# One function table for exponential and logarithm, and a state-space stage that carries a state from block to block

## The chip, the cores and the metric

The kernel runs on one core of a Trainium2 chip. It is one program of 33,089 instructions. The metric is the device time in microseconds, the median of several runs. The kernel before took 2977.17 us (three runs, 2975.21 to 2984.87). The execution that the hardware profiler recorded took 2977.9 us, and its span, from the first instruction to the last, is 2976.1 us. Engines are named as in the profile: PE (TensorE, matrix products), PEld (its weight loads), DVE (VectorE), ACT (ScalarE), POOL (GpSimd), SP (SyncE, which asks for the transfers).

## The reference, cut to what matters

Three blocks run one after the other on 512 tokens of width 1024: attention with a gated network, a convolution with a retention layer, and a block that has an mLSTM branch and a state-space branch. The change touches the state-space branch in its structure, and in the others only where exponentials and logarithms are taken. The state-space branch has 16 heads of width 64 in 4 groups, and a state of 128:

```python
def ssd_chunked(x, dt, A, Bm, Cm):          # x (B,T,16,64), dt (B,T,16), Bm/Cm (B,T,4,128)
    xc = x * dt[..., None]                  # all in chunks of tokens
    a_cs = jnp.cumsum(dt * A, -1)           # within a chunk
    cb = jnp.einsum('bclgn,bcsgn->bgcls', Cc, Bc)
    mix = cb[:, :, None] * segsum_exp(a)    # exp(a_cs[l] - a_cs[s]) for s <= l, else 0
    y_diag = jnp.einsum('bgrcls,bcsgrp->bclgrp', mix, xc)
    decay_to_end = exp(a_cs[..., -1:] - a_cs)
    states = jnp.einsum('bcsgn,bcsgrp->bcgrpn', Bc, xc * decay_to_end[..., None])
    # h_prev of a chunk = exp(a_cs[-1]) * h_prev of the one before + its states
    y_off = jnp.einsum('bclgn,bcgrpn->bclgrp', Cc, h_prev) * exp(a_cs)[..., None]
    return y_diag + y_off
# then y + d_skip * x, and the rest of the branch
```

Softmax, the stick-breaking weights (a softplus, so a logarithm of one plus an exponential), every norm (the inverse root is taken as exp(-0.5 log v)) and the mLSTM gates use exponential and logarithm in turn.

## The kernel before

All activations lie in on-chip memory as 128 channels by 512 tokens, and the weights stream through. The core of the program is `weights_part` (its loops are in the function that holds lines 960 to 1119): a list of steps, each a run of weight tiles of 256 columns or a `Part`, a piece of program for some engines. Every engine walks this list in the same order. For a tile, SP asks for 1 MB of weights (L970), POOL splits it into a rounded part and a rest (L1024, L1030), PE multiplies it in three products (L1077, 48 matmuls of 512 columns), and DVE and ACT take the result out of one of two accumulators (banks 0 to 3) and free it (L1005). POOL may run two tiles ahead of PE, and PE one tile ahead of DVE and ACT.

`conv_tiles` takes a tile of the state-space input out: DVE applies four taps (L2109, L2111), ACT adds the bias and a SiLU (L2132). There are four such tiles for the values (chunks 16 to 23 of A), then the small tile of the time steps with `steps_parts`, then four tiles for the keys (B, chunks 24 to 27) and queries (C, 28 to 31). `steps_parts` is a chain between DVE and ACT (softplus, four running sums from four starting points, their rounded parts and rests).

Then comes the state-space stage between `meeting`s, points at which PE, ACT and DVE wait for each other (L162). `mamba_inputs_part` transposes the values (PE, L1922) and multiplies them by the time step (DVE, L1932, 64 instructions of 64 columns). `mamba_part` treats the 512 tokens in four key blocks of 128, and each block meets all later queries: 512, 384, 256 and 128 columns. For every head and block, PE spreads the running sums and adds the mask (L1957, L1960), ACT takes the exponential (L2000), DVE multiplies by the group's scores, which lie in banks 0 to 3 (L2010), and PE multiplies with the values (L1969, fp32). The scores of a group are L1977, the end of a head pair is L2015. The order on PE is written out by hand: the products of a head stand after the second block of the next head.

ACT holds one table of functions at a time; the program loads one (ACT_TABLE_LOAD) whenever the function at hand isn't in it. The loads of the kernel before choose one table for Exp and another for Ln.

Of the kernel before, what the change touches and what calls it, by code (L numbers as in the profile page):

```python
# [23 lines left out]
P = 128  # L24
# [20 lines left out]
CONST_SQ = ["ident", "ones", "rot", "diff_mask", "strict", "strict_neg", "neg_upper", "neg_ones", "causal_neg"]  # L45

# [566 lines left out]
class EarlyNorm:  # L613
# [42 lines left out]
    def scalar(self, act):  # L656
# [16 lines left out]
        act.activation(st.small[:, 15:16], st.eps_col(self.eps), ACT.Ln)  # L673
# [536 lines left out]
def attention_part(nc, st):  # L1210
# [120 lines left out]
    def _(act):  # L1331
# [49 lines left out]

        for h in range(SH):
            softplus(h)
            if h:
                copy_wt(2 * h - 1)
                if h % 2 == 0:
                    head_square(h // 2 - 1)
            exps(2 * h)
            if h and h % 2 == 0:
                copy_pair(h // 2 - 1)  # L1390
            attend(h)
            copy_wt(2 * h)
            exps(2 * h + 1)
            if h and h % 2 == 0:
                head_rstd(h // 2 - 1)
# [116 lines left out]
def retention_part(nc, st, t):  # L1512
# [38 lines left out]
    def _(act):  # L1551
        for h in range(RET_HEADS):
# [48 lines left out]
def gates_parts(nc, st, rows_ready):  # L1601
# [42 lines left out]
    def _(act):  # L1644
        act.wait_ge(biased, 1)
# [20 lines left out]
def mlstm_part(nc, st):  # L1666
# [74 lines left out]
    def _(act):  # L1741
# [19 lines left out]

        for h in range(M_HEADS):
# [80 lines left out]
CUMSUM_AT = [(1, 0), (2, 0), (3, 0), (2, 3 * P)]  # L1843

def steps_parts(nc, st, rows_ready):

    ctx = ExitStack()
    biased, logged, rate_in, dt_in, summed, turned, free = sems(nc, ctx, "steps", "biased logged rate dt summed turned free")  # L1850
    hs = slice(0, S_HEADS)
    y, t1, one, dt, a = (st.A[hs, c, :] for c in range(5))
    part, rest = Part(ctx), Part(ExitStack())

    @part.vector
    def _(dve):
        dve.drain().then_inc(free, 1)
        dve.memset(st.Bl[:, 1:8, :].bitcast(F32), 0.0)
        dve.wait_ge(*rows_ready())
        dve.memset(one, 1.0)  # L1860
        dve.tensor_scalar(y, y, st.heads[hs, 2:3], None, ALU.add).then_inc(biased, 1)
        dve.wait_ge(logged, 1)
# [6 lines left out]
        for b, (c, at) in enumerate(CUMSUM_AT):  # L1869
            n = S - b * P  # L1870
            dve.tensor_tensor_scan(st.spare[hs, c, at:at + n], one[:, 0:n], a[:, b * P:S], 0.0, ALU.mult, ALU.add)
        dve.drain().then_inc(summed, 1)
        for b, (c, at) in enumerate(CUMSUM_AT):
            n = S - b * P
            dve.tensor_copy(st.Bl[hs, c, at:at + n], st.spare[hs, c, at:at + n])
        dve.drain()
        for b, (c, at) in enumerate(CUMSUM_AT):
            n = S - b * P
            dve.tensor_tensor(st.Bl[hs, c + 4, at:at + n], st.spare[hs, c, at:at + n],
                              st.Bl[hs, c, at:at + n].bitcast(F32), ALU.subtract)  # L1880

    @rest.vector
    def _(dve):
        dve.wait_ge(turned, 1)
        dve.tensor_scalar(st.cols[:, 0:64], st.PS[:, 6, 0:64], -1.0, None, ALU.mult)
        dve.tensor_copy(st.cols[:, 64:128], st.PS[:, 7, 0:64])

    @part.scalar
    def _(act):
        act.wait_ge(free, 1)  # L1890
# [6 lines left out]
        act.activation(t1, t1, ACT.Ln, bias=1.0).then_inc(logged, 1)  # L1897

    @rest.tensor
    def _(pe):  # L1900
        pe.wait_ge(dt_in, 1)
        pe.wait_ge(summed, 1)
        for b, (c, at) in enumerate(CUMSUM_AT):
            pe.transpose(st.PS[:, 6, 16 * b:16 * b + 16], st.spare[hs, c, at:at + P], st.ident[hs, hs])
            mm = pe.transpose(st.PS[:, 7, 16 * b:16 * b + 16], dt[:, b * P:(b + 1) * P], st.ident[hs, hs])
# [4 lines left out]
def mamba_inputs_part(nc, st):  # L1910

    ctx = ExitStack()
    turned, scaled = sems(nc, ctx, "mx", "turned scaled")
    XT = st.A[:, 0:8, :].rearrange("p (b c) n -> p b (c n)", b=NB)
    part = Part(ctx)
    @part.tensor
    def _(pe):
        for c in range(8):
            if c >= 4:
                pe.wait_ge(scaled, c - 3)  # L1920
            for b in range(NB):
                mm = pe.transpose(st.PS[:, c % 4, b * P:(b + 1) * P], st.A[:, 16 + c, b * P:(b + 1) * P], st.ident)  # L1922
# [3 lines left out]
    def _(dve):  # L1926
        for c in range(8):
            dve.wait_ge(turned, c + 1)
            for b in range(NB):
                for r in range(2):  # L1930
                    h = 2 * c + r
# [3 lines left out]
            ins.then_inc(scaled, 1)  # L1935
# [3 lines left out]
def mamba_part(nc, st):  # L1939

    ctx = ExitStack()
    cb_in, spread, exped, weighted, pv_done, pair_out = sems(nc, ctx, "mb", "cb spread exped weighted pv pair_out")
    XT = st.A[:, 0:8, :].rearrange("p (b c) n -> p b (c n)", b=NB)
    W = lambda h, b: st.spare[:, 4 * (h % 2) + b, :]
    at = lambda b: slice(b * P, S)
    R = S_HEADS // S_GROUPS
    pick = lambda h: st.ident_r[:, h:h + 1].to_broadcast([P, P])
    part = Part(ctx)
    @part.tensor
    def _(pe):  # L1950
        def spread_sums(h, b):
            n = NB * h + b
            if n >= 2:
                pe.wait_ge(exped, n - 1)
            k, c0 = CUMSUM_AT[b]
            for half_of in range(2):
                pe.matmul(st.PS[:, 4 + n % 2, at(b)], pick(h),  # L1957
                          st.Bl[:, k + 4 * half_of, c0:c0 + S - b * P],
                          start=(half_of == 0), stop=False, skip_group_check=True)
            pe.matmul(st.PS[:, 4 + n % 2, b * P:(b + 1) * P], st.ident_r, st.causal_neg_r,  # L1960
                      start=False, stop=True, skip_group_check=True).then_inc(spread, 1)

        def values(h):
            c, half = h // 2, slice(64 * (h % 2), 64 * (h % 2) + 64)
            if h % 2 == 0 and c >= 2:
                pe.wait_ge(pair_out, c - 1)
            for b in range(NB):
                pe.wait_ge(weighted, NB * h + b + 1)
                mm = pe.matmul(st.PS[half, 6 + c % 2, at(b)], XT[:, b, h * 64:(h + 1) * 64], W(h, b)[:, at(b)],  # L1969
                               start=(b == 0), stop=(b == NB - 1), skip_group_check=True)  # L1970
            mm.then_inc(pv_done, 1)

        def group_products(g):
            for b in range(NB):
                if g:
                    pe.wait_ge(weighted, NB * R * g)
                pe.matmul(st.PS[:, b, at(b)], st.A[:, 24 + g, b * P:(b + 1) * P], st.A[:, 28 + g, at(b)],  # L1977
                          start=True, stop=True).then_inc(cb_in, 1)

        for h in range(S_HEADS):
            if h % R == 0:
                if h:
                    values(h - 1)
                group_products(h // R)
            for b in range(NB):
                spread_sums(h, b)
                if b == 1 and h % R:
                    values(h - 1)
        values(S_HEADS - 1)  # L1990

    @part.scalar
    def _(act):
        for h in range(S_HEADS):
            for b in range(NB):
                n = NB * h + b
                act.wait_ge(spread, n + 1)
                if h >= 2:
                    act.wait_ge(pv_done, h - 1)
# [571 lines left out]
```

## Time and profile before

| | |
|---|---|
| median of 3 runs | 2977.17 us |
| profiled execution | 2977.9 us |
| its span | 2976.1 us |
| PE busy | 2678.5 us, 90% |
| POOL / DVE / ACT busy | 51% / 45% / 24% |
| mean granted clock of TensorE | 0.94 |

Busy is the time in which an engine worked on something. The granted clock is given as a share of 2.4 GHz; in the records it is either 1.0 or 0.5 (1.2 GHz), and a stretch shows the mean. A chain of waits goes back from the last instruction, at each step to what released it. "L1077" is line 1077 of the program above.

### The profile page before, as it was taken

What the parts mean: (1) busy time and instruction counts of PE and PEld (TensorE: products, weight loads), DVE (VectorE), ACT (ScalarE), POOL (GpSimd) and SP (SyncE); (2) the same over time, 40 slices, a digit from 0 to 9 for tenths busy, and PEclk for the clock granted to TensorE, in tenths of its full rate; (3) what the DMA queues carried; (4) which work ended last, traced back from release to release, by engine and by line L of the source; (5) the groups of instructions that cost most, each with busy time, mean ns of one, the idle gap of its engine ahead of it and who ended that gap; (6) DMA issues with size and microseconds to landing.
All of it is one profiled execution on the core that took longest, in us unless ns stands there. A gap on an engine that the chain in (4) does not pass through costs nothing. (4 is left out here: it accounts for less than half of the span.)

```text
span 2976.1 us, 33089 instructions
## 1 busy us (share of the span) xinstructions
PE 2678.5 (90%) x11848; PEld 2094.8 (70%) x11848; DVE 1349.7 (45%) x1959; ACT 702.5 (24%) x1044; POOL 1522.4 (51%) x1030
## 2 busy tenths in 40 slices
PE   6897779999999997799988988989988989899997
PEld 5784447888877775588946865868865768678774
DVE  4963435122259999668013315241264213544352
ACT  2002652011153333420031114141023230300002
POOL 1543006576678886367514734407650347466551
PEclk7997889999999999899999999889999999999998
DMA  7531002233322221123121322203330122223320
GB/s 253 188 114 64 0 1 71 86 98 99 99 77 93 85 85 56 35 97 99 57 71 43 99 58 59 70 14 99 86 85 15 43 71 90 66 89 95 99 74 29
DMA packets 230481, 231.28 MB, mean 78 GB/s; under 512 B 9995, under 2 KB 228844, under 8 KB 230252
## 3 DMA queue, kind: packets, MB, share of 16 engines
q1 hardware_dynamic: 225968, 228.74, 24.5%
q10 hardware_dynamic: 4412, 1.24, 0.2%
q8 instruction: 58, 0.95, 0.1%
q14 instruction: 43, 0.35, 0.0%
HBM read 227.86 MB, written 2.10 MB: 77 GB/s over the span
## 5 line engine op out<-in xcount | busy, mean ns | idle before, releaser
L1030 POOL TENSOR_TENSOR Wl<-raw,Wh 128x512 fp32r<-128x512 f32 (+3 forms) x772 | 1035.2, 1372 | 29.1 <-issue 1.3
L1024 POOL TENSOR_SCALAR Wh<-raw 128x2048 fp32r<-128x2048 f32 (+3 forms) x197 | 368.6, 1872 | 1307.0 <-PE PS L1077 1039.4
L1077 PE MATMUL PS<-Hh,Wh 128*128 128x512 f32 x2056 | 819.5, 399 | 108.4 <-DVE Hl L596 36.4
L1077 PE MATMUL PS<-Hl,Wh 128*128 128x512 f32 x2056 | 813.2, 396 | 0.0
L1077 PE MATMUL PS<-Hh,Wl 128*128 128x512 f32 x2056 | 812.2, 395 | 0.0
L1077 PEld LDWEIGHTS PS<-Hh,Wh 128*128 128x128 f32 x2056 | 390.7, 190 | 216.0 <-issue 78.3
L1077 PEld LDWEIGHTS PS<-Hh,Wl 128*128 128x128 f32 x2056 | 390.2, 190 | 87.8 <-issue 1.5
L1077 PEld LDWEIGHTS PS<-Hl,Wh 128*128 128x128 f32 x2056 | 391.0, 190 | 83.2
L1077 PE MATMUL PS<-Bh,Wh 128*128 128x512 f32 x688 | 271.9, 395 | 17.9 <-DVE Bl L2059 9.1
L1077 PE MATMUL PS<-Bl,Wh 128*128 128x512 f32 x688 | 270.4, 393 | 0.0
L1077 PE MATMUL PS<-Bh,Wl 128*128 128x512 f32 x688 | 270.3, 393 | 0.0
L2218 DVE SCALAR_TENSOR_TENSOR PS<-spare,PS 128x512 f32<-128x512 f32 x368 | 252.1, 751 | 9.1 <-ACT PS L2176 2.4
L1077 PEld LDWEIGHTS PS<-Bh,Wh 128*128 128x128 f32 x688 | 130.8, 190 | 50.1 <-issue 12.9
L1077 PEld LDWEIGHTS PS<-Bh,Wl 128*128 128x128 f32 x688 | 130.7, 190 | 27.5
L1077 PEld LDWEIGHTS PS<-Bl,Wh 128*128 128x128 f32 x688 | 130.9, 190 | 27.0
L1077 PE MATMUL PS<-Wh,Hh 128*128 128x256 f32 x512 | 145.0, 283 | 1.8 <-POOL Wl L1030 1.8
L1077 PE MATMUL PS<-Wh,Hl 128*128 128x256 f32 x512 | 144.9, 283 | 0.0
L1077 PE MATMUL PS<-Wl,Hh 128*128 128x256 f32 x512 | 144.9, 283 | 0.0
L1161 DVE SCALAR_TENSOR_TENSOR X<-X,PS 128x512 f32 (+1 forms) x64 | 41.1, 684 | 225.9 <-PE PS L1077 225.5
L2111 DVE SCALAR_TENSOR_TENSOR A<-PS,params,A 128x510 f32 (+4 forms) x160 | 112.4, 744 | 15.9 <-issue 15.6
L2109 DVE TENSOR_SCALAR A<-PS,params 128x512 f32 (+1 forms) x68 | 47.9, 745 | 148.6 <-PE PS L1077 148.2
L1077 PEld LDWEIGHTS PS<-Wh,Hh 128*128 128x128 f32 x512 | 98.3, 192 | 2.1 <-POOL Wl L1030 2.0
(359 smaller groups left out, 2953.9 us busy)
## 6 DMA issues: line engine op xcount, KB each, us to landing
raw<-in_w_in SPq DMA_DIRECT2D x44, 1024.0 KB, 6.0
raw<-in_w_ff SPq DMA_DIRECT2D x32, 1024.0 KB, 5.3
raw<-in_conv_w_in SPq DMA_DIRECT2D x24, 1024.0 KB, 5.2
raw<-in_ret_w_in SPq DMA_DIRECT2D x24, 1024.0 KB, 5.2
spare<-in_ada_w SPq DMA_DIRECT2D x20, 1024.0 KB, 6.8
raw<-in_w_up SPq DMA_DIRECT2D x20, 1024.0 KB, 5.4
raw<-in_w_out SPq DMA_DIRECT2D x8, 1024.0 KB, 5.2
raw<-in_conv_w_out SPq DMA_DIRECT2D x8, 1024.0 KB, 5.2
```

The lines of the kernel that those rows point to most:

```text
L1024: pool.tensor_scalar(st.Wh[0:rows, slot, k, 0:g.width], st.raw_slot(slot)[0:rows, k, 0:g.width], 1.0, 1.0, ALU.mult, ALU.mult)
L1030: ins = pool.tensor_tensor(st.Wl[0:rows, slot, k, 0:g.width], st.raw_slot(slot)[0:rows, k, 0:g.width], st.Wh[0:rows, slot, k, 0:g.width].b ...
L1077: mm = pe.matmul(out, lhs, rhs, start=(k == 0 and n == 0), stop=(k == parts[-1][0] and n == 2))
L1161: ins = e.scalar_tensor_tensor(x, x, x_scale, a, ALU.mult, ALU.add)
L2109: ins = e.tensor_scalar(out[0:m, b, :], acc[0:m, b, :], w, None, ALU.mult)
L2111: ins = e.scalar_tensor_tensor(out[0:m, b, back:S], acc[0:m, b, 0:S - back], w, out[0:m, b, back:S], ALU.mult, ALU.add)
L2218: e.scalar_tensor_tensor(s, U[:, b, k:k + S], wts[:, k, b:b + 1], s, ALU.mult, ALU.add)
```

## The change

The program now names a table that holds both exponential and logarithm, and asks for it (`preload_act_table_set`) ahead of attention, the early norms, retention, both gate computations, the mLSTM and the group norm. The state-space branch is written anew. The running sum restarts at each block of 128 tokens, so a block meets only its own queries through the weights (128 x 128 for each head), and what came before it arrives through a state (128 x 1024) that is carried over three block ends. The values are now the moving operand of the products, 64 columns each, and the result, tokens by channels, is transposed back. The input transposes stand in two halves between weight tiles, the time-step tile comes ahead of the value tiles, and one of the three meetings goes.

```diff
-        act.activation(st.small[:, 15:16], st.eps_col(self.eps), ACT.Ln)
+        act.preload_act_table_set(EXP_AND_LOG)          # "natural_log_exp_and_others"
...
     # steps_parts, DVE
-        dve.memset(st.Bl[:, 1:8, :].bitcast(F32), 0.0)
+        dve.memset(st.Bl[:, 0, :].bitcast(F32), 0.0)
...
-        for b, (c, at) in enumerate(CUMSUM_AT):
-            dve.tensor_tensor_scan(st.spare[hs, c, at:at + n], one[:, 0:n], a[:, b * P:S], 0.0, ALU.mult, ALU.add)
+        dve.tensor_tensor_scan(total, one, a, 0.0, ALU.mult, ALU.add)
...
     # mamba_inputs_part, DVE
-                    ins = dve.tensor_scalar(XT[:, b, h * 64:(h + 1) * 64],
-                                            st.PS[:, c % 4, b * P + 64 * r:b * P + 64 * r + 64],
-                                            st.cols[:, 64 + 16 * b + h:65 + 16 * b + h], None, ALU.mult)
+            dve.tensor_tensor(XT[:, :, c * P:(c + 1) * P].rearrange("p b (r n) -> p b r n", r=2),
+                              st.PS[:, 4 + c % 4, :].rearrange("p (b r n) -> p b r n", b=NB, r=2),
+                              dt[:, :, 2 * c:2 * c + 2].unsqueeze(3).to_broadcast([P, NB, 2, 64]),
+                              ALU.mult).then_inc(scaled, 1)
...
+    def state(pe, b):
+        pe.wait_ge(xd_in, b + 1)
...
+        for g in range(S_GROUPS):
+            mm = pe.matmul(S_NEW[:, 4 * g * 64:4 * (g + 1) * 64], BT[b][:, g * P:(g + 1) * P],
+                           XD[b][:, 4 * g * 64:4 * (g + 1) * 64], start=True, stop=True)
...
+    @front.gpsimd
+    def _(pool):
+        pool.wait_ge(*x_done)
+        for b in range(NC):
+            if b == 2:
+                pool.wait_ge(s_in, 1)
+            pool.tensor_tensor(heads_of(XD[b]), heads_of(XT[:, b, :]),
+                               left[:, b, :].unsqueeze(2).to_broadcast([P, S_HEADS, 64]), ALU.mult).then_inc(xd_in, 1)
...
+        def spread_sums(h):
+            if h >= 2:
+                pe.wait_ge(exped, h - 1)
+            pe.matmul(st.PS[:, h % 2, :], pick(h), rows, start=True, stop=False)
+            pe.matmul(st.PS[:, h % 2, :], st.ident_r, st.causal_neg_r.unsqueeze(1).to_broadcast([P, NB, P]),
+                      start=False, stop=True).then_inc(spread, 1)
...
+        for c in range(8):
+            if c < 7:
+                spread_sums(2 * c + 2)
+                spread_sums(2 * c + 3)
+            if c < 2:
+                values(c)
+            if c == 0:
+                state(pe, 2)
+            if c:
+                from_before(c - 1)
+            if c >= 2:
+                back(c - 2)
+                values(c)
...
+        act.activation(STATE[0], S_NEW, ACT.Copy).then_inc(state_in, 1)
         for h in range(S_HEADS):
...
+            for q in range(NB):
+                ins = act.activation(W(h)[:, q * P:(q + 1) * P], st.PS[:, h % 2, q * P:(q + 1) * P], ACT.Exp,
+                                     bias=st.cols[:, 16 * q + h:16 * q + h + 1])
...
+        def join(c):
+            dve.wait_ge(crossed, c + 1)
+            dve.wait_ge(pv_done, 2 * c + 2)
...
     # fourth_steps
-                conv_tiles(st, w3, H, 4, at_xbc, 16, "sc", "s_conv_b_3", S_CONV),
                 dt_rows, steps,
-                conv_tiles(st, w3, H, 4, at_xbc + D, 24, "sc", "s_conv_b_3", S_CONV, first=KC), steps_rest,
-                *apart(nc, "mamba", mamba_inputs_part(nc, st), mamba_part(nc, st))]
+                values, steps_rest,
+                keys[0], inputs[0], keys[1], inputs[1], queries[0], turn, queries[1], front,
+                *apart(nc, "mamba", mamba)]
```

`values(c)` in PE's program is 8 matmuls of 64 columns (fp32, two heads, four blocks), `from_before(c)` 3 of 128 columns against the carried states, `back(c)` 4 transposes. On DVE `keep(g)` copies a group's scores out of PSUM, `weight(h)` multiplies the exponentials by them, `next_state(b)` decays a state and adds the new one, `join(c)` adds the two parts of a head pair in three instructions, and `skip(c)` is what L2015 was.

The inner order of the stage on PE. Before, in the middle of a group (L1957 and L1960 spread and mask one block of one head, L1969 is the product of the head before it):

```order
L1969 MATMUL PS<-spare,A 64x512
L1969 MATMUL PS<-spare,A 64x384
L1969 MATMUL PS<-spare,A 64x256
L1969 MATMUL PS<-spare,A 64x128
L1957 MATMUL PS<-Bl,round_sq 128x256 x2
L1960 MATMUL PS<-round_sq 128x128
L1957 MATMUL PS<-Bl,round_sq 128x128 x2
L1960 MATMUL PS<-round_sq 128x128
L1957 MATMUL PS<-Bl,round_sq 128x512 x2
L1960 MATMUL PS<-round_sq 128x128
L1957 MATMUL PS<-Bl,round_sq 128x384 x2
L1960 MATMUL PS<-round_sq 128x128
```

And PE now, one head pair (L2028 and L2029 spread and mask a whole head, L2052 is `from_before`, L2061 `back`, L2041 `values`):

```order
L2028 MATMUL PS<-Bl 128x512
L2029 MATMUL PS<-round_sq 128x512
L2028 MATMUL PS<-Bl 128x512
L2029 MATMUL PS<-round_sq 128x512
L2052 MATMUL PS<-spare,A 128x128 x3
L2061 MATMUL PS<-squares,A 128x128 x4
L2041 MATMUL PS<-A,spare 128x64 x8
```

The 7 rows of the second piece are two heads; the 12 rows of the first are one.

DVE in the same place before (L1932 is the end of the input stage, L2010 multiplies by the scores in PSUM):

```order
L1932 TENSOR_SCALAR A<-PS,cols 128x64 x64
L2010 TENSOR_TENSOR spare<-spare,PS 128x512
L2010 TENSOR_TENSOR spare<-spare,PS 128x384
L2010 TENSOR_TENSOR spare<-spare,PS 128x256
L2010 TENSOR_TENSOR spare<-spare,PS 128x128
L2010 TENSOR_TENSOR spare<-spare,PS 128x512
```

And DVE now, one head pair (L2116 is `weight`, its scores now in A; L2133 to L2138 are `join`, L2144 `skip`):

```order
L2116 TENSOR_TENSOR spare<-spare,A 128x512
L2116 TENSOR_TENSOR extra<-extra,A 128x512
L2133 TENSOR_TENSOR A<-PS,spare 128x3x128
L2136 COPY A<-PS 128x128
L2138 TENSOR_TENSOR A<-A,PS 128x3x128
L2144 SCALAR_TENSOR_TENSOR A<-A,skip,PS 128x512
```

A head has one multiplication of 512 columns where it had four of 1280 in all, and each pair has three instructions that were not there.

ACT in attention, the second head, before (L1337 to L1341 the softplus, L1366 a copy, L1359 the softmax's exponentials):

```order
L1337 ACTIVATE spare<-PS 128x1280
L1339 ACTIVATE spare<-spare 128x1280
L1341 ACT_TABLE_LOAD
L1341 ACTIVATE spare<-spare 128x1280
L1366 ACTIVATE A<-PS 128x256
L1359 ACT_TABLE_LOAD
L1359 ACTIVATE A,cols<-PS,cols 128x384 x2
```

and now:

```order
L1340 ACTIVATE spare<-PS 128x1280
L1342 ACTIVATE spare<-spare 128x1280
L1344 ACTIVATE spare<-spare 128x1280
L1369 ACTIVATE A<-PS 128x256
L1362 ACTIVATE A,cols<-PS,cols 128x384 x2
```

Both loads of a head are gone. In the whole program there were 81 rows of loads on ACT, and there are 38.

## Rows read from the trace of the kernel before

**Rows 1.** the busy shares, from the page's part 1.

```profile
PE 2678.5 (90%) x11848; PEld 2094.8 (70%) x11848; DVE 1349.7 (45%) x1959; ACT 702.5 (24%) x1044; POOL 1522.4 (51%) x1030
```

**Rows 2.** stretches: length, busy time by engine, granted clock, DMA share, GB/s.

```profile
2232.00:2248.00 16.00, 6.91 (x33) 5.47 (x34) 12.68 (x66) 1.22 (x2) 0.35 (x1) 0.71 0.22 66
2248.00:2334.00 86.00, 79.97 (x353) 49.79 (x352) 33.60 (x72) 32.32 (x66) 0.00 (x0) 0.99 0.00 1
```

**Rows 3.** the chain of waits through the stage: start us, us, engine and line.

```profile
2200.75 24.43 PE PS L1077 x96
...
2234.55 10.25 DVE A L1932 x53
...
2247.01 3.97 PE PS L1977 x8
...
2260.60 2.30 PE PS L1969 x8
...
2263.43 0.48 ACT spare L2000
2263.95 0.73 PE PS L1957 x2
...
2333.73 66.47 PE PS L1077 x292
```

**Rows 4.** groups by shape, 2225 to 2340 us: busy us, mean ns | idle before.

```profile
L1969 PE MATMUL PS<-spare,A 128*64 128x512 f32 x32 | 17.2, 618 | 0.0
...
L2010 DVE TENSOR_TENSOR spare<-spare,PS 128x512 f32<-128x512 f32 x16 | 11.0, 688 | 28.8 <-ACT spare L2000 28.8
...
L1922 PE MATMUL PS<-squares,A 128*128 128x128 f32 x32 | 5.9, 347 | 9.8 <-ACTq L162 7.5 <-DVE A L1932 2.3
L2000 ACT ACTIVATE spare<-PS,cols 128x128 f32<-128x128 f32 x16 | 5.8, 361 | 0.0
```

**Rows 5.** instructions of PE in order of time, the mLSTM stage.

```profile
1930.79 4.67 PE L1714 MATMUL PS<-A,spare 128*128 128x129 f32 x20
...
1939.77 2.50 PE L1714 MATMUL PS<-A,spare 128*128 128x129 f32 x20
...
1975.03 0.60 PE L1723 MATMUL PS<-squares,A 128*128 128x128 f32 x4
...
1986.63 3.93 PE L1723 MATMUL PS<-squares,A 128*128 128x128 f32 x16 [5.76 <-DVE A L1802]
```

**Rows 6.** instructions of DVE in order of time, where the steps are computed.

```profile
2173.66 3.04 DVE L1858 MEMSET Bl<- 128x3584 f32 x1 [1.17 <-issue]
...
2194.43 1.39 DVE L2109 TENSOR_SCALAR A<-PS,params 128x512 f32 x2
```

**Rows 7.** who waited for whom, 2160 to 2202 us: total, times, longest.

```profile
PE PS L1077 <- DVEq L1005: 5.3, 1, 5.3
...
PE PS L1077 <- POOL Wl L1030: 1.9, 1, 1.9
```

**Rows 8.** instructions of ACT in order of time, the attention stage.

```profile
300.27 1.27 ACT L1339 ACTIVATE spare<-spare 128x1280 f32<-128x1280 f32 x1
301.60 1.28 ACT L1341 ACT_TABLE_LOAD   x1
302.89 1.27 ACT L1341 ACTIVATE spare<-spare 128x1280 f32<-128x1280 f32 x1
```

**Rows 9.** instructions of DVE in order of time, the attention stage.

```profile
304.19 1.49 DVE L1407 SCALAR_TENSOR_TENSOR spare<-PS,spare 128x1280 f32<-128x1280 f32 x1 [0.79 <-ACT spare L1341]
...
325.19 1.49 DVE L1407 SCALAR_TENSOR_TENSOR spare<-PS,spare 128x1280 f32<-128x1280 f32 x1 [1.89 <-ACT spare L1341]
```

**Rows 10.** stretches of the span, the attention stage; columns as in Rows 2.

```profile
257.00:430.00 173.00, 130.65 (x509) 79.72 (x507) 64.83 (x171) 103.34 (x154) 8.23 (x7) 0.84 0.04 13
```

**Rows 11.** DVE in order of time in retention, POOL idle.

```profile
1521.59 2.49 DVE L1571 TENSOR_TENSOR A<-A 128x512 f32<-128x512 f32 x4
```

**Rows 12.** one line of the kernel, DVE, beside a busy POOL: ns min/median/max.

```profile
L1003 DVE TENSOR_TENSOR Bl<-A,Bh x20: 1224/2214/2375, 515.9 to 2040.0; 128x1024 f32 x16, 128x1024 fp32r<-128x1024 f32 x4
```

More of the change, by code:

```diff
@@ L1839, in mlstm_part @@
     return part
-CUMSUM_AT = [(1, 0), (2, 0), (3, 0), (2, 3 * P)]
 def steps_parts(nc, st, rows_ready):
     ctx = ExitStack()
-    biased, logged, rate_in, dt_in, summed, turned, free = sems(nc, ctx, "steps", "biased logged rate dt summed turned free")
+    biased, logged, rate_in, dt_in, summed, ended, decayed, turned, free, cols_in = sems(
+        nc, ctx, "steps", "biased logged rate dt summed ended decayed turned free cols")
     hs = slice(0, S_HEADS)
-    y, t1, one, dt, a = (st.A[hs, c, :] for c in range(5))
+    y, t1, one, dt, a, total, grown, left = (st.A[hs, c, :] for c in range(8))
     part, rest = Part(ctx), Part(ExitStack())
+    rest.cols_in = cols_in
     @part.vector
@@ L1861, in _ @@
         dve.tensor_scalar(y, y, st.heads[hs, 2:3], None, ALU.add).then_inc(biased, 1)
+        dve.drain()
+        dve.memset(one.rearrange("h (b n) -> h b n", b=NB)[:, :, 0:1], 0.0)
         dve.wait_ge(logged, 1)
@@ L1897, in _ @@
         act.activation(t1, t1, ACT.Ln, bias=1.0).then_inc(logged, 1)
+        act.wait_ge(summed, 1)
+        act.activation(grown, total, ACT.Exp)
+        act.wait_ge(ended, 1)
+        act.activation(left, left, ACT.Exp)
+        act.drain().then_inc(decayed, 1)
     @rest.tensor
@@ L1973, in group_products @@
[L1973 to L1989, printed above, removed]
@@ new lines, in from_before, with back @@
+        def from_before(c):
+            if c < 2:
+                pe.wait_ge(kept, c + 3)
+                pe.wait_ge(state_in, NC)
+            else:
+                pe.wait_ge(joined, c - 1)
+            for q in range(1, NB):
+                mm = pe.matmul(cross(c)[:, (q - 1) * P:q * P], st.A[:, 28 + c // 2, q * P:(q + 1) * P],
+                               STATE[q - 1][:, c * P:(c + 1) * P], start=True, stop=True)
+            mm.then_inc(crossed, 1)
+        def back(c):
+            pe.wait_ge(joined, c + 1)
+            if c >= 2:
+                pe.wait_ge(out_in, c - 1)
+            for q in range(NB):
+                mm = pe.transpose(st.PS[:, 6 + c % 2, q * P:(q + 1) * P], XT[:, q, c * P:(c + 1) * P], st.ident)
+            mm.then_inc(turned, 1)
@@ new lines, in skip @@
+        def skip(c):
+            dve.wait_ge(turned, c + 1)
+            dve.scalar_tensor_tensor(st.A[:, 16 + c, :], st.A[:, 16 + c, :], st.skip[:, c:c + 1],
+                                     st.PS[:, 6 + c % 2, :], ALU.mult, ALU.add).then_inc(out_in, 1)
+        keep(0)
+        keep(1)
+        weight(0)
+        weight(1)
+        next_state(1)
+        keep(2)
+        keep(3)
+        weight(2)
+        weight(3)
+        next_state(2)
+        join(0)
+        for c in range(2, 8):
+            weight(2 * c)
+            weight(2 * c + 1)
+            join(c - 1)
+            skip(c - 2)
@@ L2020, in group_norm_part @@
+        join(7)
+        skip(6)
+        skip(7)
+    return turn, front, part
 def group_norm_part(nc, st, src, gain, hi, lo, src_ready):
@@ L2511, in fourth_steps @@
             steps, steps_rest = steps_parts(nc, st, dt_rows.all_staged)
+            values = conv_tiles(st, w3, H, 4, at_xbc, 16, "sc", "s_conv_b_3", S_CONV)
+            keys, queries = ([conv_tiles(st, w3, H, 1, at_xbc + D + (2 * k + n) * TW, 24 + 4 * k + 2 * n, "sc",
+                                         "s_conv_b_3", S_CONV, first=KC + 4 * k + 2 * n) for n in range(2)]
+                             for k in range(2))
+            first_inputs = mamba_inputs_part(nc, st, "mx0", 0, values.act_ready, (steps_rest.cols_in, 1))
+            inputs = first_inputs, mamba_inputs_part(nc, st, "mx1", 4, values.act_ready, first_inputs.done)
+            turn, front, mamba = mamba_parts(nc, st, lambda g: keys[g // 2].act_ready(0), inputs[1].done)
             return [
```

205 lines of the change are left out of this document (136 added, 69 removed).

## The prediction

> **What bounds the kernel now.** The page's busy shares come first: PE works 90% of the span and no other engine much more than half of it [rows 1]. What isn't PE's own work is therefore in the places where PE waits or runs at its lower clock, and the change has to be read there. The stretches show the state-space branch: its input stage (2232 to 2248 us) has PE busy for 6.9 of 16 us, with DVE at 12.7, while in the main stage (2248 to 2334 us) PE is busy for 80 of 86 us at a granted clock of 0.99 [rows 2]. So the first is a DVE stage and the second a PE stage. The chain of waits says the same: 10.25 us in a row on DVE L1932, then from 2247.01 us on pieces of PE, with a short ACT piece of 0.48 us between two PE pieces where PE waited for a free bank [rows 3]. From the end of the last query tile (2200.75 + 24.43 = 2225.2 us) to the first weight product of the next tile (2333.73 us) PE does 108.5 us without weights. The reader should see that a stage bound by PE shrinks with PE's work, and only until DVE or ACT takes over.
>
> **The main stage, engine by engine.** The column counts fall: per head and block PE had 512 + 384 + 256 + 128 = 1280 columns of fp32 value products, and twice that in spreading. Now each block meets itself only.
>
> PE now. An fp32 product is two records in the profile. 20 records of 129 columns took 2.50 us at full clock, 0.125 us each [rows 5], and four transposes 0.60 us, 0.15 each [rows 5]. A rounded product of 512 columns costs 66.47/292 = 0.228 us [rows 3]. The new work: spreading 32 x 0.228 = 7.3; scores 32 records x 0.125 = 4.0; two state products of four times 256 columns, 16 records at twice 0.125, 4.0; the part from before, 48 records, 6.0; transposes back, 32 x 0.15 = 4.8; values, 128 records of 64 columns. These last have no row. At half of 0.125 they cost 8, at the full 0.125, if the weight load is what limits them, 16; I take 0.09, nearer to the full one, 11.5. Sum 37.6 us (34 to 42).
>
> DVE now. An instruction of 512 columns takes 0.69 with an operand in PSUM [rows 4] and 2.49/4 = 0.62 with both in SBUF [rows 11]. Four copies 2.8; 16 weightings 9.9; two states with two instructions of 1024 columns, twice 2 x 1.24, 5.0; eight joins of two times 384 and once 128 columns, by columns 0.52 + 0.52 + 0.3, 10.7; eight last additions 5.5. Sum 34, and 26 drains at some 0.1 us, which is my estimate from the gaps between such instructions: 36.5 us.
>
> ACT now. 64 exponentials of 128 columns, at most 0.361 us each [rows 4], 23 us, and a copy. It isn't the bound.
>
> So PE and DVE are nearly level. In a head pair PE does about 0.9 + 0.75 + 0.6 + 1.4 = 3.7 us and DVE 1.2 + 1.3 + 0.7 + 0.3 = 3.5 us, and each has work of the next pair queued while the other joins: the pairs run at about 3.7 us. Ahead of the first join stand the state's copy on ACT, a table load of 1.28 [rows 8], the first exponentials, the four copies and both state steps, together about 13 us on DVE; then seven pairs, 26; then the last join, turning back and last addition, 2.5. That is 41.5. Three additions: PE has been idle for most of 8 us before, and after such a gap it runs at its lower clock, where the 20 records took 4.67 instead of 2.50 us [rows 5]: some 7 us of the stage at half speed, +3.5. POOL is busy at the start of the stage, because its splitting of the next two tiles now stands behind the three state inputs, where it used to be done before (POOL 0.00 in rows 2); DVE instructions with two SBUF operands suffer then: L1003, 1024 columns, takes 2.21 in the median and 1.22 at best [rows 12]. Six weightings and the two scalings of the state in that time, +4. The hand-over at the end, +1. The main stage is then 50 us, against 2333.7 - 2247.0 = 86.7 now: **36.7 us less**.
>
> The Trainium skill, page "SBUF — State Buffer", section "Who interferes with whom", says that a DVE instruction with two SBUF inputs and a GpSimd instruction that reads SBUF exclude each other for the whole instruction. The rows agree that such DVE instructions take 1.8 times as long; taken strictly, each of the eight could wait out a whole POOL instruction, and the +4 would be about +10. This is the fifth case below.
>
> **The input stage.** It took 2247.0 - 2234.5 = 12.5 us and goes from the path whole. What it issued isn't gone: 32 transposes now stand between the key and query tiles on PE, 32 x 0.15 = 4.8 us, with 12 more for the keys, 1.8, and 8 more small ones, 0.8. DVE's eight new instructions (512 columns, 2.8 us for each half) stand behind the taps of a tile, four pairs of instructions like the one of 1.39 us [rows 6], with their pauses about 6.5 us of DVE, per 48 x 0.228 = 10.9 us of PE: 9.3 of 10.9, hidden, and 1.6 us a tile is the cover that is left. One meeting and the first four transposes go: 2234.5 - 2225.2 = 9.4 becomes 8.2.
>
> **The time steps.** Today their chain on DVE starts at 2173.66 with 3.04 us of clearing and ends at 2194.43 [rows 6], and PE, with both accumulators full, waits 5.3 us for it [rows 7] and then runs at the lower clock (96 products in 24.43 us instead of 96 x 0.228 = 21.9). Now the chain has one sum instead of four, a small clearing, and one load less, about 10 us, and it starts two tiles earlier, when both accumulators are free: both losses go, 5.3 + 2.5 = 7.8. The wait for POOL behind the short tile, 1.9 [rows 7], only moves. Against the 4.8 + 1.8 + 0.8 above this is +0.4.
>
> The restructured branch therefore gives 36.7 + 12.5 + 1.2 + 0.4 = **50.8 us**.
>
> **The tables.** A load takes 1.28 us, and there are 43 fewer in the order. They count only where somebody waits for ACT. In attention [rows 8, 9], after the logarithm of an even head DVE starts 0.8 us later than it could (idle before L1407, 0.79), of an odd head from the third on 1.9 (1.89; there the two loads of the head norm stand ahead as well), the first head gives the load whole, and the end one and a bit: 1.3 + 3 x 0.8 + 3 x 1.9 + 1.5 = 10.9. The loads ahead of the softmax are hidden under PE's suffix sums. The stage's clock is 0.84 [rows 10], and with shorter gaps some of it comes back: 2. At the end of the mLSTM PE waits 5.76 us for DVE, which waits for ACT with two loads [rows 5]: 2.6, and 1.3 in its middle. One load each at the ends of two early norms, of retention, in the group norm and in the norm behind it: 5 x 1.28 = 6.4. The third early norm has PE busy over it. Sum 10.9 + 2 + 3.9 + 6.4 = **23.2 us**; from below 9, if the waits are filled by the next engine in line, from above 31, if the clock stays up.
>
> The page "ScalarE: Activation LUTs" of the Trainium skill, section "What ACT_TABLE_LOAD costs", puts a drain of about 1.38 us beside a load of 1.28. In this trace the exponential ends at 301.54, the load runs from 301.60 to 302.88, and the logarithm starts at 302.89 [rows 8]: no such drain. By the page the table term would be nearly twice 21, by the rows it is what stands above.
>
> **Sum.** 2977.9 - 50.8 - 23.2 = 2903.9, forecast **2904 us**. The profiled execution is 0.7 us above the median of 2977.17, so nothing is corrected for it.
>
> **The rivals.**
> 1. PE stays at the lower clock. With gaps in each pair the new stage could look like attention (0.84) or worse, where it is 0.99 today [rows 2, 10]. At half clock the pair is 6.5 us on PE instead of 3.7, seven of them +20, so 2925. For: PE and DVE alternate. Against: PE is busy nearly all of each pair.
> 2. The loads are off the path. DVE and PE chains beside them end just as late, and the tables give 8: 2919. Against: the idle times in rows 9 name ACT.
> 3. Both terms larger: 64-column records cost half and attention's clock recovers: 4 + 8 + 7 less, 2885.
> 4. Slower than before: DVE reads its broadcast operands (the step, the decays, one number for 64 columns) at a much lower rate. No row shows such an operand. They are 4096 + 3072 + 2048 columns, 18 times 512. At 0.69 they are in the sum; the whole gain of 74 is gone from 0.69 + 74/18 = 4.8 us per 512 columns, and at 5.5 the time is about 2990. Against: nothing but the missing row speaks for it.
> 5. POOL and DVE exclude each other, +6: 2910.
> 6. Nothing changes: the terms cancel by a slower stage and hidden loads.
>
> **How the numbers follow.** Chances: forecast 0.61 (its own range 2891 to 2916), rival one 0.15, two 0.09, three 0.07, five 0.05, four 0.02, six 0.01. The range from 2884 to 2929 holds the forecast, one, two, three and five. A measurement of this kernel can tell about 0.3%, 9 us, from no change; all cases but four and six lie beyond that on the fast side: faster 0.97, same 0.01, slower 0.02.
>
> **What would show it.** In the profile after, the stretch between the last query tile and the next weight product should be 57 to 60 us, PE and DVE both above 70% busy in it; L1947 (the inputs) at 0.7 us each under PE's tiles; no wait of PE for L1005 near the time steps; L2041 at 0.06 to 0.125 us per record; POOL busy for the first 10 us of the stage with L2116 longer there; the idle before L1407's successor in attention gone. It is wrong if the stage's granted clock is below 0.85, if L2133 is far over 0.55 us, or if attention is less than 8 us shorter.

## The result, and the profile after

The changed kernel takes 2911.88 us in the median of 4 runs (2906.29 to 2912.49), beside 2979.02 for the kernel before on the same chip: a ratio of 0.9769, 95% interval 0.9748 to 0.979. That is some 67 us less; the forecast was 74 less, 2904. Below, the profiled executions are compared, spans of 2976.1 and 2910.4 us, 65.7 apart.

First the busy shares, from the page of the changed kernel:

```profile
PE 2647.4 (91%) x11814; PEld 2093.1 (72%) x11814; DVE 1338.6 (46%) x1885; ACT 636.0 (22%) x1004; POOL 1531.5 (53%) x1033
```

Then four stretches of its trace: length, busy time of PE, weight loads, DVE, ACT and POOL, then granted clock, DMA share, GB/s. They are attention, the mLSTM stage, the hand-over behind the last query tile, and the new main stage.

```profile
253.50:430.00 176.50, 134.35 (x513) 80.79 (x513) 67.69 (x178) 78.09 (x136) 11.44 (x9) 0.81 0.04 12
1897.70:1984.00 86.30, 74.20 (x272) 50.60 (x273) 40.51 (x121) 30.79 (x110) 13.77 (x10) 0.72 0.17 49
2217.70:2225.00 7.30, 1.69 (x9) 1.15 (x7) 5.62 (x8) 1.33 (x2) 5.39 (x4) 0.99 0.00 0
2225.00:2269.30 44.30, 40.27 (x288) 37.26 (x288) 35.63 (x56) 19.80 (x67) 12.11 (x8) 0.96 0.17 49
```

From the last query tile to the next weight product it is now 2217.7 to 2269.3 us, 51.6, where it was 108.5: 56.9 less, and shorter than the 57 to 60 us that the prediction named as its sign. In the main stage PE is busy 91% of the time and DVE 80%, as two engines that are nearly level look. The chain of waits through it (start us, us, engine and line):

```profile
2227.07 2.40 PE PS L2066 x16
2229.49 0.69 DVE A L2111
2230.31 0.69 DVE spare L2116
2231.00 1.67 DVEq L2124
2232.67 2.23 DVE spare L2122
2234.98 1.22 DVE spare L2126
...
2247.10 0.29 PE PS L2028
2247.39 0.23 PE PS L2029
2247.62 0.23 PE PS L2028
2247.86 0.23 PE PS L2029
2248.09 0.67 PE PS L2052 x6
2248.75 0.44 PE PS L2061 x4
2249.19 1.73 PE PS L2041 x16
2250.92 0.28 PE PS L2028
```

From 2229.5 to 2244 us it runs mostly through DVE (copy of scores, weighting, the two state steps), then through PE: one head pair from 2247.10 to 2250.92 is 3.82 us, and 1.73 us of it are the 16 value records of 64 columns, 0.108 each; the six of 128 columns at L2052 took 0.67 us, 0.11 each, so that half the columns saved nothing. These rows stand where [rows 3] had 3.97 and 2.30 us pieces of the old products. By shape, behind the first bar busy us and mean ns of one, then the idle time before:

```profile
L2116 DVE TENSOR_TENSOR spare<-spare,A 128x512 f32<-128x512 f32 x12 | 9.0, 776 | 0.4
...
L2133 DVE TENSOR_TENSOR A<-PS,spare 128x384 f32<-128x384 f32 x8 | 4.4, 554 | 2.3 <-PE PS L2052 2.3
...
L2122 DVE TENSOR_TENSOR spare<-spare 128x1024 f32<-128x1024 f32 x2 | 3.5, 1762 | 0.0
...
L2111 DVE COPY A<-PS 128x512 f32<-128x512 f32 x4 | 2.8, 691 | 5.5 <-PE PS L2066 5.1
```

L2133 reads the broadcast decays at 554 ns for 384 columns, what 384 columns cost in the old stage too (L2010, 548 ns), and L1947, which reads the broadcast time step, takes 681 ns for 512: rival four is out. The answer to [rows 10] is the first stretch above. The same two stages of the kernel before, attention and mLSTM:

```profile
253.80:435.80 182.00, 133.90 (x513) 81.34 (x513) 66.96 (x178) 107.46 (x159) 11.43 (x9) 0.82 0.04 12
1909.20:1991.60 82.40, 66.69 (x272) 43.12 (x272) 40.52 (x121) 36.12 (x114) 13.79 (x10) 0.79 0.18 52
```

Attention went from 182.0 us to 176.5, and its clock is still 0.81. The mLSTM stage has become longer, 86.3 us for 82.4, at a clock of 0.72 in place of 0.79.

Who PE waited for in attention, changed kernel (total us, times, longest):

```profile
PE PS L1298 <- DVEq L1415: 22.5, 8, 7.2
PE PS L1275 <- ACT A L1369: 11.8, 16, 1.3
```

and the same of the kernel before:

```profile
PE PS L1272 <- ACT A L1366: 25.2, 16, 4.0
PE PS L1295 <- DVEq L1411: 13.5, 5, 7.5
```

With the small ones PE waits 49.3 us there now and 55.1 before: only 5.8 less, though ACT has 23 instructions fewer (159 and 136), its loads of 1.28 us. When ACT no longer holds PE at L1275, PE reaches L1298 earlier and waits there for DVE's masks instead. DVE's own idle time ahead of that addition, which the prediction counted, is gone; PE's wait mostly isn't.

By stage, the 65.7 us are: branch 56.9, attention 5.5, mLSTM stage -3.9, all the rest 7.2. The forecast had 50.8 (0.4 of it at the time steps, which lie in the rest), 12.9, 3.9 and 6.4.

### The profile page after: what moved, and what is told of

It is laid out like the page before. It is cut to its first block and busy times, and to the rows that moved or that the text cites. A ratio compares the mean times of both kernels' runs of the same rounds, so it can differ in the third digit from the quotient of the medians.

```text
span 2910.4 us, 32742 instructions
## 1 busy us (share of the span) xinstructions
PE 2647.4 (91%) x11814; PEld 2093.1 (72%) x11814; DVE 1338.6 (46%) x1885; ACT 636.0 (22%) x1004; POOL 1531.5 (53%) x1033
## 5 line engine op out<-in xcount | busy, mean ns | idle before, releaser
L2261 DVE SCALAR_TENSOR_TENSOR A<-PS,params,A 128x510 f32 (+5 forms) x160 | 112.4, 744 | 14.3 <-issue 13.1
```

Of the source, the lines that this page charges most:

```text
L2261: ins = e.scalar_tensor_tensor(out[0:m, b, back:S], acc[0:m, b, 0:S - back], w, out[0:m, b, back:S], ALU.mult, ALU.add)
```

## The experiments

In all of them a stage's low clock is read from its row: a mean granted clock of 0.81 over 176.5 us is 2 x 0.19 x 176.5 = 67 us at 1.2 GHz, the rest at 2.4. Ratios are to the kernel before on the same chip.

### The two parts apart

tables_alone: the kernel before with the seven requests.

```
-        act.activation(st.small[:, 15:16], st.eps_col(self.eps), ACT.Ln)
+        act.preload_act_table_set(EXP_AND_LOG)
...      (and six more requests, as in the change)
```

> The kernel before, with the seven requests for the common table and nothing of the new branch. Theory (the tables gave little, because the next engine in line filled most of each wait): the sum of what the two traces show outside the branch, about 9 us less than before, so about 2969; attention about 5 to 6 us shorter, the mLSTM stage not shorter, or up to 4 us longer. Rival (the 23 us of the prediction were right and the branch gave only 43): about 2955, attention 11 to 13 us shorter.

Measured: 2956.42 us (2948.03 to 2964.94), ratio 0.9927 (0.9905 to 0.995), 18 us less by the medians and 22 by the ratio. The rival was nearer, though attention is 9.3 us shorter in its trace and not 11 to 13. branch_alone is the changed kernel with these seven edits undone:

> The changed kernel without the seven requests for the common table: the new branch alone. Theory: the branch gave 57 us, so about 2921, 9 us above the changed kernel. Rival (tables 23): about 2935, 23 us above the changed kernel. If the two parts help each other (clock, phase), both alone give less than their share of the 66.

Measured: 2924.21 us (2923.37 to 2930.07), ratio 0.9827 (0.9807 to 0.9847), 51 us less (45 to 57). So the branch is worth about what was forecast in the whole, though its stage is 56 us shorter: the profiled execution gives some of it back further on (from the norm behind the output projection to the last norm it was 382.0 us, 378.9 before, with more low clock). On top of the branch the tables gave 12 us by the medians; by the ratios, which compare each kernel with the one before on its own chip, 17 (9 to 26 with both intervals). Together: tables 12 to 22, by where and how they are measured; my first theory, 9, had taken one execution for the rule.

### One stage without its request

```
-        act.preload_act_table_set(EXP_AND_LOG)
         for h in range(M_HEADS):       # mlstm_plain; in attention_plain: for h in range(SH)
```

> The changed kernel without the request ahead of the mLSTM stage, whose trace has become 3.9 us longer with it. Theory (the stage's waits fall at other moments, and the clock is low in more of it): 2908, some 4 us under the changed kernel, with the stage at 84 us and a granted clock of 0.80 in place of 88 and 0.73. Rival (the stage is longer because of what lies ahead of it, and the request itself saves the 3.9 us of the prediction): 2916, the stage at 90 us or more.

> The changed kernel without the request ahead of the attention stage. Theory (the stage is 5 to 6 us shorter by it and no more): 2917 to 2918. Rival of the prediction (11 us of waits and 2 us of clock): 2925. A second rival: the loads are wholly hidden there and the 5 us come from elsewhere: 2912.

Measured: mlstm_plain 2905.68 us, ratio 0.9758 (0.9738 to 0.9778); attention_plain 2910.18, ratio 0.9778 (0.9757 to 0.9799). Neither is told apart from the changed kernel's 0.9769 by its time: by the ratios attention's request is worth 3 us, with 9 either way. The traces say more. Attention in tables_alone, mlstm_plain (both with the request) and attention_plain (without):

```profile
251.70:424.40 172.70, 130.59 (x513) 78.85 (x513) 67.73 (x178) 78.15 (x136) 11.45 (x9) 0.84 0.04 13
```

```profile
253.90:423.70 169.80, 127.60 (x513) 76.91 (x513) 67.71 (x178) 78.26 (x136) 11.47 (x9) 0.86 0.04 13
```

```profile
253.50:435.60 182.10, 134.04 (x512) 81.46 (x513) 66.89 (x178) 107.42 (x159) 11.39 (x9) 0.82 0.04 12
```

Up to the end of attention mlstm_plain and the changed kernel are the same program, and PE waits 49.3 us in both, yet the stage takes 169.8 us in one execution and 176.5 in the other: 47 and 67 us of low clock. In seven traces with the request it was 168.8, 169.8, 171.1, 172.7, 176.5, 177.7 and 177.8, mean 173.5; in three without, 181.9, 182.0 and 182.1. The request saves 4 to 13 us there, and where in this range an execution falls goes with the clock: six of the seven traces are of programs that are the same up to there, and they span the whole range. The mLSTM stage in mlstm_plain and attention_plain:

```profile
1895.70:1977.90 82.20, 66.70 (x273) 43.06 (x273) 40.26 (x121) 36.18 (x114) 13.78 (x10) 0.79 0.18 52
```

```profile
1902.00:1981.80 79.80, 67.61 (x272) 45.91 (x272) 40.74 (x121) 30.81 (x110) 13.78 (x10) 0.79 0.18 53
```

At the same clock of 0.79 the request makes it 2.4 us shorter; at 0.72 (the changed kernel's profile) it is 4.1 longer. "The request made it longer" was a wrong reading of one execution; PE's waits there fell from 15.6 to 11.8 us, nearly the 3.9 forecast. But the forecast gain isn't there on the average either: over seven traces with the request and without added work the stage took 73.9 to 86.3 us, mean 81.0, at clocks of 0.84 to 0.72; over three without it, 82.2 to 82.4.

### Work for PE in its waits

The added instructions turn (transpose) the identity matrix; nobody reads what they write.

```
+            if h and b == 0:                       # mlstm_fill, ahead of a head's first score
+                for _ in range(5): pe.transpose(st.PS[:, 7, 0:P], st.ident, st.ident)
...
+            if h == GROUP:                         # and ahead of the last four turnings
+                for _ in range(20): pe.transpose(st.PS[:, 0, 0:P], st.ident, st.ident)
```

```
+                for _ in range(10 if h % 2 else 5):   # attention_fill, ahead of suffix_sums(h)
+                    pe.transpose(TURNED[:, 0:P], st.ident, st.ident)
```

> The changed kernel; in the mLSTM stage PE turns the identity five times at the start of each head from the second on, and 20 times ahead of the last four heads' turning back, into a bank that nobody reads, where it waited for DVE 0.92 us a head and 3.9 us at the end. Theory (the clock is low in 34 to 48 us of this stage because of these waits; PE's work in them keeps it up): the stage falls from 80 to 86 us to about 72, its clock from 0.73 to over 0.95, the whole to about 2901. Rival (the clock has other reasons, the added work only costs): 30 to 40 transposes at 0.15 or 0.30 us beyond the waits, the stage 1 to 5 us longer, 2912 to 2917.

> The changed kernel; in attention PE turns the identity ten times ahead of the suffix sums of an odd head and five times of an even one, where it waited 2.8 and 1.3 us. Theory: the low clock in this stage, 47 to 67 us in the three traces that have the common table, goes down to some 20 us, the stage from 170 to 177 us to about 162, the whole to about 2900. Rival (the other waits of a head, ahead of the head's weighted values and behind the logits, suffice to bring it down, or it has other reasons): low clock as before, the stage the same or up to 5 us longer, 2910 to 2917.

Measured: mlstm_fill 2894.83 us, ratio 0.9716 (0.9695 to 0.9736); attention_fill 2891.61, ratio 0.9713 (0.9695 to 0.9731). Both theories of the clock held. The mLSTM stage of the first, and attention of the second:

```profile
1898.80:1966.90 68.10, 61.07 (x327) 41.53 (x327) 42.48 (x121) 30.88 (x110) 13.98 (x10) 0.97 0.21 62
```

```profile
256.90:415.30 158.40, 122.30 (x567) 76.42 (x568) 67.61 (x178) 78.10 (x136) 11.50 (x9) 0.93 0.04 14
```

86.3 us at 0.72 became 68.1 at 0.97. One head of the mLSTM in mlstm_fill; the dummy turnings are L1703:

```profile
1938.53 0.76 PE L1703 MATMUL PS<-squares 128*128 128x128 f32 x5
1939.50 1.12 PE L1706 MATMUL PS<-A 64*128 64x512 f32 x2 [0.21 <-DVE spare L1842]
1940.56 0.73 PE L1713 MATMUL PS<-Bh,round_sq 128*128 128x512 f32 x2
1941.22 0.91 PE L1706 MATMUL PS<-A 64*128 64x384 f32 x2
1942.06 2.50 PE L1723 MATMUL PS<-A,spare 128*128 128x129 f32 x20
```

and the same place of the changed kernel:

```profile
1953.24 1.12 PE L1703 MATMUL PS<-A 64*128 64x512 f32 x2 [0.78 <-DVE spare L1836]
1954.29 0.72 PE L1710 MATMUL PS<-Bh,round_sq 128*128 128x512 f32 x2
1954.94 1.49 PE L1703 MATMUL PS<-A 64*128 64x384 f32 x2
1956.36 4.67 PE L1720 MATMUL PS<-A,spare 128*128 128x129 f32 x20
```

The dummies fill 0.76 us of a wait of 0.8 to 0.9, and the 20 records take 2.50 us instead of 4.67. The head falls from 9.8 to 6.8 us. The Trainium skill, page "TensorE: Matmul & The Clock Gate", section "A second HAM failure mode: psum-queue depth-cycling", describes a clock that swings because PE idles shortly and often between groups; here it did so with waits of 0.8 to 1.5 us, one a head: in that stage's 86.3 us the granted clock fell to 1.2 GHz eight times, in the trace of mlstm_fill once.

### The buffer and the inputs

```
-    XD = [pair_of(a, 2) for a in (0, 2, 0)]
+    XD = [pair_of(0, 2), pair_of(2, 2), st.extra[:, :, :].rearrange("p c n -> p (c n)")]
...
-            if b == 2:
-                pool.wait_ge(s_in, 1)
```

> The changed kernel; the third state input has a buffer of its own, so that POOL doesn't wait for the first state product and splits the next two tiles before the main stage of the branch. Theory (POOL beside DVE costs about what the longer instructions show, 0.5 us for each of the first weightings and 1.1 us for the first scaling of the state): L2116 at 0.69 us throughout, the stage 2 to 3 us shorter, 2909. Rival one (they exclude each other for whole instructions, waits included): 6 us, 2906. Rival two (the start of the stage is bound by the chain through ACT and PE, DVE waits there anyway): no change.

Measured: 2905.41 us, ratio 0.9761 (0.9747 to 0.9775), too near 0.9769 to tell by time. By shape, the weightings and the state scaling in its trace:

```profile
L2114 DVE TENSOR_TENSOR spare<-spare,A 128x512 f32<-128x512 f32 x16 | 10.3, 686 | 0.4
...
L2120 DVE TENSOR_TENSOR spare<-spare 128x1024 f32<-128x1024 f32 x2 | 2.4, 1217 | 0.0
```

Against 776 and 1762 ns with POOL beside them; from the last query tile to the next weight product 49.9 us against 51.6. So POOL cost 1.7 us on the path, not the 4 of the sum nor the 10 of rival five.
```
-                keys[0], inputs[0], keys[1], inputs[1], queries[0], turn, queries[1], front,
+                keys[0], keys[1], queries[0], queries[1], *inputs, turn, front,
```

> The changed kernel; the two halves of the inputs stand behind the last query tile again, in front of the keys' turning. Theory of the prediction in its strict form (12.5 us of the input stage were saved by the place): 12 us more, 2924. Rival (half of it was the form: eight instructions of 512 columns take 0.69 us each, where 64 of 64 columns took 12.7 us; at the end of the tiles the eight would cost 6 to 7 us): 2918 to 2919. The new form hides nothing if the time doesn't change.

Measured: 2914.55 us, ratio 0.9789 (0.9771 to 0.9807), 6 us above the changed kernel's by the ratio, and the two intervals overlap. The edit puts the keys' turning (L1997) behind the last tile as well. DVE in its trace, an instruction of the second half of the inputs:

```profile
2219.91 0.69 DVE L1947 TENSOR_TENSOR A<-PS,cols 128x512 f32<-128x512 f32 x1 [1.21 <-PE PS L1940]
```

All eight stand between 2216.2 and 2223.2: 7 us. So the form, 8 instructions in place of 64, took 5.5 of the 12.5 us by itself. What the place is worth stays less certain: from the last query tile to the next weight product this execution took 68.5 us (2210.2 to 2278.7), 16.9 more than the changed kernel, of which 6.9 come back in the stretch ahead, mostly because the turnings no longer stand between the tiles. That is 10 us net, more than the 7 that remained: POOL's inputs and the keys' turning come late too, and the clock in the stretch is 0.85. By the ratios it is 6. Between the theory's 12 and the rival's 6 to 7 these runs do not decide.

### What bounds a pair

```
-                for q in range(NB):
+                for q in range(NB if r == 0 or c < 2 else 1):
                     mm = pe.matmul(inner(c)[:, q * P + 64 * r:...
```

> The changed kernel; of every odd head from the fifth on PE computes the values of the first block only, 3 of 4 products left out (its output is incomplete): 6 records of 0.108 us less in each of six pairs. If PE bounds the pairs (3.82 us each), they fall by 0.65 us to 3.2, the stage by 3.9 us, to 2908. If DVE bounds them, nothing changes, 2912; if both are level, as the prediction has it (3.7 and 3.5), the pair falls to DVE's 3.5 or 3.6, 1.5 to 2 us in all.

The kernel leaves out 3 of 4 value products of every odd head from the fifth on. Measured: 2898.2 us (2886.39 to 2914.91), ratio 0.9749 (0.972 to 0.9778). Its chain of waits in the pairs:

```profile
2227.04 0.47 DVE A L2133
2227.50 0.20 DVE A L2136
2227.78 0.56 DVE A L2138
2228.46 0.13 DVE A L2144
2228.59 0.53 issue
2229.12 0.69 DVE spare L2116
2229.81 0.60 DVEq L2137
2230.41 0.47 DVE A L2133
```

The chain has moved to DVE whole, and a pair (L2133 to L2133) takes 3.37 us, 0.45 less for 0.65 us of PE taken away: the two were level within half a microsecond, PE ahead. From the first join to the last it is 21.75 us, 1.5 less than in the changed kernel, as the expectation had it for level engines. Its profiled execution is 25.8 us shorter in all, and that is mostly the clock of two stages which the edit doesn't touch: attention 7.7 (168.8 us), mLSTM 12.4 (73.9 us at 0.84).

### All edits that gained, and the tables at a held clock

fills_and_buffer is mlstm_fill, attention_fill and own_buffer (whose own gain no time shows) in one kernel; fills_own_tables is the same without the requests ahead of attention and of the mLSTM stage.

> The changed kernel with the three edits that gained: PE's added turnings in attention and in the mLSTM stage, and the buffer of its own for the third state input. If they add up (16 to 17 for each fill, 2 to 3 for the buffer): about 2875, with attention at 158 and mLSTM at 68 us. Rival (the low clock moves to other stages, which have waits of their own, and takes part of it back): 2885.

> The kernel with the three edits, without the requests for the common table in attention and mLSTM: what the tables are worth where the clock is held up. Theory of the prediction (10.9 us of waits in attention, 2.6 and 1.3 in the mLSTM stage): 13 to 15 us more, 2889, the two stages at 169 and 71 us. Rival (another chain ends just as late): 5 to 6 us more in all, 2881. If the loads' waits themselves bring the clock down again, more than 15.

Measured: fills_and_buffer 2875.25 us (2873.08 to 2878.1), ratio 0.9652 (0.9639 to 0.9666): the gains add (0.0053, 0.0056 and 0.0008 apart, 0.0117 together), and the low clock doesn't come back elsewhere. Without the two requests 2901.26, ratio 0.9741 (0.9726 to 0.9755), 26 us more. Attention and mLSTM stage of the latter:

```profile
253.60:432.50 178.90, 133.98 (x568) 85.77 (x568) 66.96 (x178) 107.51 (x159) 11.41 (x9) 0.85 0.04 12
1899.10:1973.60 74.50, 65.13 (x328) 43.78 (x328) 38.91 (x121) 36.23 (x114) 13.86 (x10) 0.91 0.19 57
```

and with the requests:

```profile
254.10:414.10 160.00, 123.83 (x568) 77.65 (x568) 67.74 (x178) 78.19 (x136) 11.53 (x9) 0.92 0.04 14
1882.00:1950.90 68.90, 61.34 (x328) 41.12 (x328) 43.30 (x121) 30.89 (x110) 13.91 (x10) 0.98 0.21 62
```

18.9 and 5.6 us, above both forecasts; the third case that was put, that the loads' waits bring the clock down again, held (0.85 and 0.91). Of the 18.9 us, 10.2 are PE's own work, longer at the lower clock (133.98 for 123.83), and the rest is waits. A last kernel adds to fills_and_buffer 24 turnings in each of seven long waits:

```
+        for _ in range(24):      # behind the last sum of squares of a norm (TOTAL), and so in two more places
+            pe.transpose(TOTAL[:, 0:P], st.ident, st.ident)
```

> The kernel with the three edits (2875), and 24 more turnings of the identity, 3.1 us at full clock, where PE waits for one long chain: behind the last sum of squares of each of the five full norms (waits of 5 to 11 us), at the end of attention (4.8) and behind the first state product (5.6). Theory (each of these waits brings the clock down for 7 to 14 us, and shorter ones don't): some 30 of the 60 us of low clock behind them go, 8 to 15 us less, 2860 to 2867. Rival (the rest of each wait, 2 to 8 us, still brings it down, only later): no change, 2875, or a few us more where the turnings run at half clock beyond the wait.

Measured: 2872.65 us (2869.86 to 2877.49), ratio 0.9637 (0.9618 to 0.9655). The rival was nearer. By the mean granted clock of the profiled executions (0.957 for 0.954) the low clock fell from 264 us to 247, 17 where the theory had 30, and the time by 3 us by the medians, 4 by the ratios: 3 us of work in a wait of 5 to 11 us leaves most of the low clock where it was. The intervals of this kernel and the one before it overlap; both beat the changed kernel.

## Why the prediction was right

The branch was forecast at 50.8 and is 56.9 us in its trace, 51 in the whole. The tables were forecast at 23.2; they gave 18 to 22 on the old kernel and 12 to 17 on the new. That the profiled total came so near is in part luck: a branch stage that gained more than forecast stood against an attention and an mLSTM stage that gained less.

- **Main stage, 50 forecast, 44.3.** The terms of PE were right but for two sizes. The values' records, with no row to go by, took 0.108 us, not 0.09: 13.8 instead of 11.5. The turning back took 0.11 a piece, not 0.15: 3.5 instead of 4.8. The pair came at 3.82 for 3.7 in the middle of the stage, and DVE right under it at 3.37 for 3.5. What was too large are the additions. Up to the first join (L2133, 2242.8) it took 17.8 us, where 13 and the surcharges for clock and POOL, 7.5, made 20.5. The low clock lasted 3.5 us of the stage (0.96 of 44.3), not 7, at its start, where PE's pieces are on the chain (L2066 in 2.40 us; the same line later took 1.78 at full clock in own_buffer), and so cost under 2 us, not 3.5; POOL cost 1.7, not 4. And seven pairs at 3.7 make 26, where the joins stood 23.25 us apart from first to last: the first two pairs were partly done ahead of the first join, the last have nothing to spread.
- **Input stage, hand-over, time steps.** 9.4 became 7.3 (8.2 forecast). PE no longer waits for DVE at the steps, as forecast, and L1947 takes 0.68 us under PE's tiles. These are the steps that held as put.
- **Attention, 12.9 forecast, 5.5 in the profile, 8.5 in the mean of seven traces.** This is the step that failed, and by the prediction's own sign (wrong if attention is less than 8 us shorter) the profile says so. The 10.9 us were read from DVE's idle time ahead of the add [rows 9]; what counts is PE's, and PE's waits fell by 5.8, since the wait for ACT at one place became a wait for DVE at the next. That was rival two, in one stage. The 2 us for the clock were right in sign only on the mean: the stage swings by 9 us from one execution to the next. With the clock held up by other means the same requests are worth 18.9 us, which a sum over waits can't give.
- **mLSTM stage, 3.9 forecast, -3.9 in the profile.** The waits fell by the forecast amount (15.6 to 11.8). The clock took 7.7 back in this execution, and in the mean of seven 2.5 (81.0 us, 1.4 less than before); the sum had no term for that.
- **The other loads, 6.4 forecast, 7.2.** Right in the sum, and in part by luck: between attention and the mLSTM stage, where three loads or 3.8 us were counted, it is 5.7, and behind the branch, where two or 2.6 were counted, 1.3. The 1467.7 us between the two stages were 1464.1 to 1472.0 in other traces with all requests ahead of them. No run takes one of these loads by itself.

The low clock was rival one, placed in the new stage, where it stayed at 0.96. It acted in the two old stages that wait in short pieces.

## What to carry to other kernels

Before pricing shorter waits of another engine, look at PE's own waits and at the granted clock of the stage: where PE pauses shortly and often, the clock and not the wait can be the larger term, and its size differs between executions of one program, so that one trace doesn't price it. A few matmuls on data at hand, into a bank that nobody reads, shorter than the wait they stand in, can then gain in one stage what taking instructions out did in the whole kernel (16 to 20 us a stage here, against 12 to 22 for 44 table loads fewer, 99 before and 55 after). Where two engines are level, count the pair once by the larger, and don't add surcharges that fall on the engine which isn't setting the end at that moment.

## What was not expected of the hardware

- A turning of a resident 128x128 operand cost 0.15 us a piece in the fills (five in 0.76), and the turning back in the pairs 0.11 (four in 0.44), where rows of the old kernel had 0.60 for four [rows 5]; the pieces of a chain leave out the overlap with the next instruction, a group's busy time does not. So the 0.15 of the sum was the wrong price for a chain, not a turning that became cheaper.
- The granted clock of one stage, same instructions, stood at 0.81 in one execution and 0.86 in another, 6.7 us apart; without the request three executions agreed within 0.2 us. Why one form of the loop is steady and the other is not stays open.
